# A scan step of 22 rounds in place of 23 in a two-layer attention and RWKV kernel

## The chip, the cores and the metric

The kernel runs on one core of a Trainium2 chip. The metric is the device time in microseconds (us) of one launch; a figure for a kernel is the median of several launches. The engines are TensorE (PE for matmuls, PEld for its weight loads), VectorE (DVE), ScalarE (ACT), GpSimd (POOL) and SyncE (SP), each working through its own list in order; between them stand semaphores. Matmuls write to eight banks of PSUM (`ps`), everything else lies in SBUF.

## What is computed

Two blocks follow each other over 1040 tokens of width 1024. The first has two layers, each with multi-head attention (4 heads), a bidirectional RWKV recurrence of 8 heads of 64, and a mixture of experts; the second has differential attention, a gated MLP and a dense feed-forward part. The change touches the recurrence alone:

```
def _wkv_scan(r, decay, k, v, kk, a, reverse):
    def step(S, inp):
        r_t, w_t, k_t, v_t, kk_t, b_t = inp
        sa = jnp.einsum('bhvk,bhk->bhv', S, kk_t)
        S = S * w_t[:, :, None, :] - sa[..., None] * b_t[:, :, None, :] + v_t[..., None] * k_t[:, :, None, :]
        return S, jnp.einsum('bhvk,bhk->bhv', S, r_t)
...
    def direction(d, wd, ad, reverse):
        wl = w0[d] + jnp.tanh(wd) @ w2[d]
        decay = jnp.exp(-jnp.exp(-jax.nn.softplus(-wl) - 0.5))
        a = jax.nn.sigmoid(a0[d] + ad @ a2[d])
        kd = heads(k * (1.0 + (a - 1.0) * k_a))
        y = _wkv_scan(rh, heads(decay), kd, vh, kk, heads(a), reverse)
        bonus = jnp.sum(rh * kd * r_k, -1, keepdims=True) * vh
        return y, bonus
```

It runs once forward (direction 0) and once backward (direction 1) in each layer, and the attention of the same layer is worked between its pieces.

## The kernel before

The recurrence is not run token by token. A step takes 104 tokens (two chunks of 52) of all 8 heads; `NT` is 10, so each direction has 10 steps. A step is cut into phases 0 to 31, written out for each engine in `scan_pe`, `scan_act`, `scan_dve` and `scan_pool`:

- phases 0 to 5: two small products (line 1366), tanh on ACT, on DVE the gate (L1541), the running sums (L1544), `cs` and `x1`; on POOL `a` and `b` (L1640, L1643);
- phases 6 to 10: on ACT the exponentials `ei`, `eK`, `ea` of the sums, on DVE `kr0`, `hb1`, `kr1`, products with them. On ACT phase 5 has the factor scaling "1+" (L1489, four instructions), which waits for POOL's `b`; POOL's `ak` (L1646) follows it;
- phase 11: TensorE turns `v` and `hb1` (`ps<-consts,u` and `ps<-consts,hb`), ACT takes them out of PSUM (`vT`, `hbT`), DVE makes `hb0`;
- phases 12 and 13: TensorE multiplies `kr` with `hb` (two banks each), DVE masks the results out of PSUM into `Ab` and `Ak`. The product of phase 12 goes to the banks that `vT` and `hbT` have left, that of phase 13 to those that `Ab` has left;
- phase 14: `hb0` is turned, and the bonus product `aa,rk`; phase 15 turns `lm` and makes T of level 0;
- phases 16 to 25: five levels. The even phase is `T,lm` on TensorE and then `XX` on DVE; the odd one is `XX,T` and `T,XX` on TensorE, and then T, half taken out by DVE (L1609), half by ACT. The next phase needs this each time;
- phases 26 to 31: the state of the two chunks (`S,kr`, `rh,T`, and the long product of 2.3 us), one after the other.

`PHASES` says which phases a round holds. A round is a stretch of code in which every engine does these phases of one direction, then the attention's share, then the phases of the other direction. Direction 1 lags by `STAGGER` = 11 rounds. A direction in its first four phases (rounds 0 to 3 of its step) stands last in the round, else direction 0 stands first:

```
    for n in range(STEPS * NT + STAGGER):
        turns_ = []
        for d in range(2):
            step, ph = divmod(n - STAGGER * d, STEPS)
            if 0 <= step < NT:
                turns_.append((ph < 4, d, step, PHASES[ph]))
        turns_.sort()
```

Rounds are counted below from 0 at the start of a step of direction 0. An attention item (one head, one tile of queries) spans six rounds, k = 0 to 5. On TensorE k = 0 is the larger part of the scores (`kn,qn`, `kpe,qp`; about 2.1 us), k = 1 the rest (0.7), k = 3 the turning of p (`consts,p`; 1.0), k = 4 the product with v (`v,pT`; 2.4). k = 1 has DVE's maxima (L1826), k = 2 three exponentials on ACT (L1811), k = 3 on DVE the taking out of pT (L1843), k = 5 on DVE the scaling `o` (L1851) and on ACT the square of it (L1815). Items start in the rounds `STARTS` = 2, 8, 13, 20 of a step of direction 0 in the first layer and in steps 0 and 5 of the second, and in `FEWER` = 2, 9, 17 in its other steps, always counted from `STEPS` times the step.

Of the kernel before, what the change touches and what calls it, by code (L numbers as in the profile page):

```python
# [9 lines left out]
ACT = mybir.ActivationFunctionType  # L10
# [268 lines left out]
def bc(ap, shape):  # L279
    return ap.to_broadcast(shape)  # L280
# [896 lines left out]

PHASES = [(0, 1, 2), (3, 4, 5), (6, 7, 9, 8, 10), (11,), (12,), (13, 14), (15,)] + [(ph,) for ph in range(16, 32)]  # L1180
STEPS = len(PHASES)
USES = 34
LEVELS = 6
# [35 lines left out]
def rounds():  # L1219
# [3 lines left out]
# [7 lines that stand above are left out]
# [9 lines left out]
def chunk(d, step):  # L1239
    i = step if d == 0 else NT - 1 - step  # L1240
    return slice(C * i, C * i + C)
# [11 lines left out]
def scan_bank(P, d, step, use):  # L1253
    return P.ps[2 * d + use % 2]
# [216 lines left out]
def scan_act(e, P, li, d, step, ph):  # L1471
    rw, pe, dv, ac, po = P.rw, P.c("scan_pe"), P.c("scan_dve"), P.c("scan_act"), P.c("scan_pool")
    m, sl, key = P.scan[d], chunk(d, step), (li, d, step)

    def take(out, view, use):
        e.wait_ge(*pe.at(*key, use))
        e.activation(out, view, ACT.Copy).then_inc(*ac.tick(*key, "ev", use))
# [5 lines left out]
        e.activation(m.aa, m.aa, ACT.Tanh, scale=0.5).then_inc(*ac.tick(*key, "aa"))  # L1483
    if ph == 11:
        take(m.vt[0:HP].rearrange("p c n -> p (c n)"), scan_bank(P, d, step, 2)[0:HP, :], 2)
    if ph == 5:
        e.wait_ge(*po.at(*key, "b"))
        for j in range(4):
            made = e.activation(m.aa[:, j, :], m.aa[:, j, :], ACT.Identity, bias=rw.par[:, 7, j:j + 1],  # L1489
                                scale=rw.par[:, 1, j:j + 1])  # L1490
        made.then_inc(*ac.tick(*key, "1+"))
    if ph == 6:
        e.wait_ge(*dv.at(*key, "x1"))
        e.activation(m.ei, m.cs if d == 0 else m.x1, ACT.Exp, scale=KAPPA).then_inc(*ac.tick(*key, "ei"))
# [2 lines left out]
            *ac.tick(*key, "eK"))  # L1497
    if ph == 8:
        e.activation(m.ea, m.cs if d == 0 else m.x1, ACT.Exp, scale=-KAPPA).then_inc(*ac.tick(*key, "ea"))
    if ph == 9:  # L1500
        e.wait_ge(*dv.at(*key, "f"))
        e.activation(m.f, m.f, ACT.Exp, scale=-0.5 * KAPPA).then_inc(*ac.tick(*key, "f"))
    if ph == 11:
# [25 lines left out]
def scan_dve(e, P, li, d, step, ph):  # L1529
    rw, pe, dv, ac, po = P.rw, P.c("scan_pe"), P.c("scan_dve"), P.c("scan_act"), P.c("scan_pool")  # L1530
    ident = bc(P.K["id52"][0:HP, :].unsqueeze(1), [HP, 8, H])
    m, sl, key = P.scan[d], chunk(d, step), (li, d, step)
# [29 lines left out]
        e.tensor_copy(m.old[:, (step + 1) % 2, :], total[:, :, m.chunks[1]]).then_inc(*dv.tick(*key, "old"))  # L1562
    if ph == 8:
        e.wait_ge(*ac.at(*key, "ei"))
        e.wait_ge(*po.at(*key, "ak"))
        e.scalar_tensor_tensor(m.hb[:, 1, :, :], m.hb[:, 1, :, :], -1.0, m.ei, ALU.mult, ALU.mult).then_inc(
            *dv.tick(*key, "hb1"))
    if ph == 9:
# [2 lines left out]
    if ph == 10:  # L1571
        e.wait_ge(*ac.at(*key, "ea"))
        e.tensor_tensor(m.kr[:, :, 1, :], rw.r[:, :, sl], m.ea, ALU.mult).then_inc(*dv.tick(*key, "kr1"))
    if ph == 11:
        e.tensor_tensor(m.hb[:, 0, :, :], m.aa, m.ei, ALU.mult).then_inc(*dv.tick(*key, "hb0"))
    if 12 <= ph < 14:
        dst = m.ab if ph == 12 else m.ak
# [57 lines left out]
def scan_pool(e, P, li, d, step, ph):  # L1635
    rw, pe, dv, ac, po = P.rw, P.c("scan_pe"), P.c("scan_dve"), P.c("scan_act"), P.c("scan_pool")
    m, sl, key = P.scan[d], chunk(d, step), (li, d, step)
    if ph == 2:
        e.wait_ge(*ac.at(*key, "aa"))
        e.tensor_scalar(m.aa, m.aa, 0.5, 0.5, ALU.mult, ALU.add).then_inc(*po.tick(*key, "a"))  # L1640
    if ph == 4:
        e.wait_ge(*po.at(*key, "a"))
        e.tensor_tensor(m.hb[:, 1, :, :], m.aa, rw.kk[:, :, sl], ALU.mult).then_inc(*po.tick(*key, "b"))  # L1643
    if ph == 7:
        e.wait_ge(*ac.at(*key, "1+"))
        e.tensor_tensor(m.aa, m.aa, rw.k[:, :, sl], ALU.mult).then_inc(*po.tick(*key, "ak"))  # L1646
    if ph == 11:
        e.wait_ge(*dv.at(*key, "hb0"))
        e.tensor_tensor(m.aa, rw.r[:, :, sl], m.aa, ALU.mult).then_inc(*po.tick(*key, "rka"))
    if ph in MASKS:  # L1650
        lv = MASKS[ph]
        if lv == 0:
            e.wait_ge(*dv.at(*key, "ev", 5))
        elif lv == 2:
            e.wait_ge(*dv.at(*key, "T", 0))
        elif lv > 2:
            e.wait_ge(*pe.at(*key, 8 + 3 * (lv - 2)))
        e.tensor_tensor(m.LM[lv % 2][0:HP], m.ab[0:HP, :, 0, :],  # L1658
                        bc(m.lmask[0:HP, H * lv:H * lv + H].unsqueeze(1), [HP, 8, H]), ALU.mult).then_inc(
            *po.tick(*key, "lm", lv))  # L1660
# [226 lines left out]
def recur_act(e, P, li):  # L1887
    for n, parts in groupby(rounds(), key=lambda x: x[0]):
        for _, part in parts:
            if part is None:  # L1890
                att_turned_act(e, P, li, n)
                att_act(e, P, li, n)
            else:
                scan_act(e, P, li, *part)
        close_head_act(e, P, li, n - STEPS * NT)
# [17 lines left out]
def recur_pool(e, P, li):  # L1913
    for n, part in rounds():
        if part is None:
            close_head_pool(e, P, li, n - STEPS * NT)
        else:
            scan_pool(e, P, li, *part)
# [2463 lines left out]
```

## Time and profile before

| | us |
|---|---|
| median of 3 runs (4924.06 to 4928.11) | 4927.36 |
| the profiled execution | 4924.1 |
| its span | 4921.9 |
| granted TensorE clock, mean share of full speed | 0.956 |
| PE busy over the span | 4475.2 (91%) |
| the scan of layer 0, about | 357 to 1070 |
| the scan of layer 1, about | 2193 to 2950 |

The profiled execution is 3.3 us faster than the median. The page gives busy times over the whole span, in which the two scans make up some 1470 us. In a timeline a matmul's end is modelled: a row of 32 matmuls of 0.60 us is followed by the next row 0.42 us after its start. A bracket behind a row gives the idle time of the engine before it, and what ended this.

### The profile page before, as it was taken

To read this page: it belongs to the slowest core of one execution; us is meant where nothing else is said; L and a number is where in the kernel's file an instruction comes from. 1 tells how busy PE (TensorE), PEld (TensorE's weight loads), DVE (VectorE), ACT (ScalarE), POOL (GpSimd) and SP (SyncE) were. 2 spreads that over 40 slices of the span, in tenths; PEclk is the share of its full clock that TensorE was granted. 3 is DMA by queue.
4 is the path that set the end of the run, shared out by engine and by line. 5 is a ranking of instruction groups with operands and counts; after the bars stand their busy time and mean duration, and the time that the engine had idled before them with its cause. 6 is when DMAs were issued, how large, how long until landed. Compare 5 with 4: busy or idle time off the path is not lost. (4 is left out here: it accounts for less than half of the span.)

```text
span 4921.9 us, 126091 instructions
## 1 busy us (share of the span) xinstructions
PE 4475.2 (91%) x55528; PEld 3810.2 (77%) x55528; DVE 3137.0 (64%) x4910; ACT 2160.1 (44%) x3962; POOL 1187.2 (24%) x863
## 2 busy tenths in 40 slices
PE   6989999989799968989999989799979988999999
PEld 6888888876588858878888877688857657888887
DVE  5436666669788874346656668788864475561752
ACT  2333443442288853433334342588843252331431
POOL 1002222222244420012222221354321000222221
PEclk9999999999799988999999999899989789999999
DMA  5421111123367664320111032566751003333332
GB/s 148 142 63 25 37 22 34 24 80 89 128 250 270 252 196 128 118 58 23 34 35 24 23 100 86 218 245 259 264 180 31 13 1 123 96 96 123 112 114 91
DMA packets 378285, 535.78 MB, mean 109 GB/s; under 512 B 117446, under 2 KB 301830, under 8 KB 349694
## 3 DMA queue, kind: packets, MB, share of 16 engines
q1 hardware_dynamic: 335645, 488.54, 30.7%
q0 software_dynamic: 40752, 33.95, 2.2%
q8 instruction: 440, 7.21, 0.6%
q10 hardware_dynamic: 1344, 5.24, 0.3%
q14 instruction: 104, 0.84, 0.1%
HBM read 569.43 MB, written 121.40 MB: 140 GB/s over the span
## 5 line engine op out<-in xcount | busy, mean ns | idle before, releaser
L289 PE MATMUL ps<-w_hi,xbT 128*128 128x512 f32 x1520 | 499.5, 400 | 19.8 <-DVE w L2838 19.8
L289 PE MATMUL ps<-hT,w_in 128*128 128x416 f32 (+1 forms) x2736 | 491.6, 338 | 4.1 <-DVE hT L3118 4.1
L289 PEld LDWEIGHTS ps<-hT,w_in 128*128 128x128 f32 x2736 | 455.6, 194 | 29.7 <-issue 19.2
L2838 DVE TENSOR_TENSOR w<-w,w_hi 128x2048 fp32r<-128x2048 f32 x190 | 425.4, 2278 | 2.2 <-issue 1.1
L1658 POOL TENSOR_TENSOR lm<-Ab,consts 116x416 f32<-116x416 f32 x240 | 254.3, 1071 | 472.6 <-PE ps L289 222.8
L289 PEld LDWEIGHTS ps<-w_hi,xbT 128*128 128x128 f32 x1520 | 289.1, 190 | 87.6 <-DVE w L2838 28.8
L2795 ACT ACTIVATE w_hi<-w 128x2048 fp32r<-128x2048 f32 x190 | 355.3, 1936 | 0.0
L289 PE MATMUL ps<-w,xbT 128*128 128x512 f32 x760 | 299.3, 394 | 0.0
L2869 DVE TENSOR_TENSOR w<-w,w_hi 128x2048 fp32r<-128x2048 f32 x95 | 221.7, 2333 | 95.5 <-ACT w_hi L2831 95.5
L289 PE MATMUL ps<-w_hi,actT 128*128 128x512 f32 x760 | 250.8, 391 | 5.0 <-DVE actT L2864 5.0
L289 PE MATMUL ps<-x1T,w_gate 128*128 128x512 f32 x1056 | 248.9, 392 | 3.0 <-DVE x1T L3805 1.6
L289 PE MATMUL ps<-x1T,w_up 128*128 128x512 f32 x1056 | 246.5, 389 | 0.0
L289 PE MATMUL ps<-w_down,act 128*128 128x512 f32 x1056 | 241.6, 391 | 3.0 <-POOL w_down L4031 3.0
L289 PEld LDWEIGHTS ps<-x1T,w_gate 128*128 128x128 f32 x1056 | 199.6, 189 | 45.5 <-issue 1.9
L289 PEld LDWEIGHTS ps<-w_down,act 128*128 128x128 f32 x1056 | 199.3, 189 | 45.0 <-POOL w_down L4031 3.4
L289 PEld LDWEIGHTS ps<-x1T,w_up 128*128 128x128 f32 x1056 | 198.2, 188 | 41.1
L289 PE MATMUL ps<-w_out,mixT 128*104 128x512 f32 (+1 forms) x864 | 220.2, 409 | 9.4 <-DVE w_out L2176 5.1
L1601 DVE TENSOR_TENSOR XX<-ps,consts 116x416 f32<-116x416 f32 x200 | 117.5, 587 | 172.4 <-PE ps L289 172.4
L4022 POOL TENSOR_TENSOR w_up<-w_up,w_up 128x1024 fp32r<-128x1024 f32 x44 | 116.4, 2645 | 459.5 <-ACT w_up L3944 459.5
L2784 POOL DMA_INDIRECT t_ys<-yo,slots x95 | 101.2, 1065 | 464.6 <-PE ps L296 374.1
L289 PEld LDWEIGHTS ps<-w_out,mixT 128*104 128x104 f32 (+1 forms) x864 | 152.6, 180 | 67.7 <-DVE w_out L2176 9.8
L795 POOL TENSOR_TENSOR w_in<-w_in,w_in 128x1024 fp32r<-128x1024 f32 x22 | 56.1, 2549 | 607.1 <-ACT w_in L810 607.1
(463 smaller groups left out, 10872.8 us busy)
## 6 DMA issues: line engine op xcount, KB each, us to landing
w<-in_moe_w_dram SPq DMA_DIRECT2D x192, 1024.0 KB
w_gate<-in_w_gate_dram SPq DMA_DIRECT2D x44, 512.0 KB, 3.8
w_up<-in_w_up_dram SPq DMA_DIRECT2D x44, 512.0 KB, 3.9
w_down<-in_w_down_dram SPq DMA_DIRECT2D x44, 512.0 KB, 3.6
w_in<-in_w_in_dram SPq DMA_DIRECT2D x36, 512.0 KB, 4.6
w_out<-in_w_out_dram SPq DMA_DIRECT2D x24, 512.0 KB, 7.4
t_h<-x SPq DMA_DIRECT2D x20, 416.0 KB
kn<-t_kn SPq DMA_DIRECT2D x8, 1040.0 KB, 6.7
```

Source lines behind the costliest of these rows:

```text
L289: made = e.matmul(out, a, b, start=start, stop=stop)
L795: e.tensor_tensor(w.lo, w.x, w.hf, ALU.subtract).then_inc(*count.tick(li, "lo", n))
L1601: e.tensor_tensor(m.XX[0:HP].rearrange("p (k u) t -> p k u t", k=2), both_banks(P, d, 0)[0:HP].rearrange("p k (u t) -> p k u t", t=H), bc( ...
L1658: e.tensor_tensor(m.LM[lv % 2][0:HP], m.ab[0:HP, :, 0, :], bc(m.lmask[0:HP, H * lv:H * lv + H].unsqueeze(1), [HP, 8, H]), ALU.mult).then_i ...
L2784: e.indirect_dma_start(T["ys"], bass.IndirectOffsetOnAxis(P.slots[:, table_column(b - 2):table_column(b - 2) + 1], 0), m.yo[b % 2], None, ...
L2795: e.activation(w.hi, w.x, ACT.Copy).then_inc(*P.c("moe_act").tick(li, "w13", b, k))
L2838: e.tensor_tensor(w.lo, w.x, w.hf, ALU.subtract).then_inc(*P.c("moe_dve").tick(li, "w13", b, k))
L2869: e.tensor_tensor(w.lo, w.x, w.hf, ALU.subtract).then_inc(*dv.tick(li, "w2", b))
L4022: e.tensor_tensor(w.lo, w.x, w.hf, ALU.subtract).then_inc(*po.tick(0, c, "lo", f))
```

## The change

`PHASES` puts phases 11 and 12 of a step into one round, so a step has 22 rounds and the whole scan of a layer 231 in place of 241. `STAGGER`, `STARTS` and `FEWER` stay as they are. On ACT the scaling "1+" moves from phase 5 behind the exponentials, to phase 10, and the exponential of `f` from phase 9 to 12. On DVE `hb1` waits for POOL's `b` and no longer for `ak`, and `hb0`, now in phase 12, waits for `ak`. POOL's `rka` moves to phase 12.

```diff
-PHASES = [(0, 1, 2), (3, 4, 5), (6, 7, 9, 8, 10), (11,), (12,), (13, 14), (15,)] + [(ph,) for ph in range(16, 32)]
+PHASES = [(0, 1, 2), (3, 4, 5), (6, 7, 9, 8, 10), (11, 12), (13, 14), (15,)] + [(ph,) for ph in range(16, 32)]
...
-    if ph == 5:
-        e.wait_ge(*po.at(*key, "b"))
-        for j in range(4):
-            made = e.activation(m.aa[:, j, :], m.aa[:, j, :], ACT.Identity, bias=rw.par[:, 7, j:j + 1],
-                                scale=rw.par[:, 1, j:j + 1])
-        made.then_inc(*ac.tick(*key, "1+"))
...
-    if ph == 9:
+    if ph == 10:
+        e.wait_ge(*po.at(*key, "b"))
+        for j in range(4):
+            made = e.activation(m.aa[:, j, :], m.aa[:, j, :], ACT.Identity, bias=rw.par[:, 7, j:j + 1],
+                                scale=rw.par[:, 1, j:j + 1])
+        made.then_inc(*ac.tick(*key, "1+"))
+    if ph == 12:
         e.wait_ge(*dv.at(*key, "f"))
         e.activation(m.f, m.f, ACT.Exp, scale=-0.5 * KAPPA).then_inc(*ac.tick(*key, "f"))
...
     if ph == 8:
         e.wait_ge(*ac.at(*key, "ei"))
-        e.wait_ge(*po.at(*key, "ak"))
+        e.wait_ge(*po.at(*key, "b"))
...
-    if ph == 11:
+    if ph == 12:
+        e.wait_ge(*po.at(*key, "ak"))
         e.tensor_tensor(m.hb[:, 0, :, :], m.aa, m.ei, ALU.mult).then_inc(*dv.tick(*key, "hb0"))
...
-    if ph == 11:
+    if ph == 12:
         e.wait_ge(*dv.at(*key, "hb0"))
         e.tensor_tensor(m.aa, rw.r[:, :, sl], m.aa, ALU.mult).then_inc(*po.tick(*key, "rka"))
```

With 22 rounds the item that starts in round 20 has its k = 2 to 5 in rounds 0 to 3 of the next step; before, k = 3 to 5 stood in rounds 0 to 2, and k = 2 in round 22. ScalarE's list at the start of direction 0's step in the first layer, before (`p` are the exponentials of k = 2, L1815 the square of k = 5, L1489 the scaling "1+"):

```order
L1811 ACTIVATE p125_174,stat127_176<-ps,stat127_176 104x416 x2
L1811 ACTIVATE p125_174,stat127_176<-ps,stat127_176 104x208
L1477 ACTIVATE T101_150<-ps 116x2x208
L1798 ACTIVATE pT126_175<-ps 104x2x104
L1481 ACTIVATE ps<-sig71_120 128x416
L1483 ACTIVATE aa74_123<-aa74_123 128x416
L1489 ACTIVATE aa74_123<-aa74_123,par11_60 128x104 x4
L1477 ACTIVATE T101_150<-ps 116x2x208
L1815 ACTIVATE pT126_175,mss5_54<-o129_178 104x128
L1494 ACTIVATE ei76_125<-cs72_121 128x416
L1496 ACTIVATE ps<-x73_122 128x416
```

The same place after:

```order
L1477 ACTIVATE T101_150<-ps 116x2x208
L1812 ACTIVATE p125_174,stat127_176<-ps,stat127_176 104x416 x2
L1812 ACTIVATE p125_174,stat127_176<-ps,stat127_176 104x208
L1481 ACTIVATE ps<-sig71_120 128x416
L1483 ACTIVATE aa74_123<-aa74_123 128x416
...
L1493 ACTIVATE ea75_124<-cs72_121 128x416
L1497 ACTIVATE aa74_123<-aa74_123,par11_60 128x104 x4
L1816 ACTIVATE pT126_175,mss5_54<-o129_178 104x128
L1477 ACTIVATE vT85_134<-ps 116x512
L1477 ACTIVATE hbT84_133<-ps 116x512
```

The exponentials of k = 2 moved from before the taking out of T to between it and the tanh, the scaling "1+" behind `ea`, and the square from before `ei` to directly before `vT`. TensorE's list behind the small products (L1366) of the same step, before:

```order
L1366 MATMUL ps<-u6_55,a213_62 128x104
L289 MATMUL ps<-T101_150,lm104_153 52x52 x16
L289 MATMUL ps<-v116_165,pT126_175 104x128 x10
L289 MATMUL ps<-XX102_151,T101_150 52x52 x16
...
L289 MATMUL ps<-consts0_49,hb83_132 52x64 x16
L289 MATMUL ps<-kr82_131,hb83_132 52x104 x16
L289 MATMUL ps<-T101_150,XX102_151 52x52 x16
L289 MATMUL ps<-kr82_131,hb83_132 52x104 x16
```

And after:

```order
L1366 MATMUL ps<-u6_55,a213_62 128x104
L289 MATMUL ps<-T101_150,lm104_153 52x52 x16
L296 MATMUL ps<-consts0_49,p125_174 104x104 x10
L289 MATMUL ps<-XX102_151,T101_150 52x52 x16
...
L289 MATMUL ps<-consts0_49,hb83_132 52x64 x16
L289 MATMUL ps<-kr82_131,hb83_132 52x104 x32
L289 MATMUL ps<-consts0_49,hb83_132 52x64 x16
L289 MATMUL ps<-aa74_123,rk814_63 8x104 x4
L289 MATMUL ps<-T101_150,XX102_151 52x52 x16
```

Between `T,lm` and `XX,T` of the other direction there stood `v,pT`, and now the turning of p; the two products of `kr` and `hb` now follow each other.

## Rows read from the trace of the kernel before

**Rows 1.** Both scans: us, busy PE PEld DVE ACT POOL, PEclk, DMA share, GB/s.
```profile
357.00:1070.00 713.00, 654.96 (x19132) 590.61 (x19131) 454.49 (x1083) 295.56 (x825) 196.42 (x196) 0.99 0.15 34
2193.00:2950.00 757.00, 677.78 (x19883) 614.78 (x19881) 476.46 (x1070) 300.54 (x814) 210.20 (x205) 0.97 0.17 43
```

**Rows 2.** Timeline, TensorE, layer 0, one step: start, us, idle before.
```profile
570.50 0.60 PE L289 MATMUL ps<-XX,T 52*52 52x52 f32 x32 [0.72 <-DVE XX L1601]
580.04 0.60 PE L289 MATMUL ps<-T,lm 52*52 52x52 f32 x32 [0.55 <-ACT T L1477]
581.80 1.10 PE L289 MATMUL ps<-consts,u 64*52 64x64 f32 x32 [0.49 <-DVE kr L1570]
586.39 1.63 PE L289 MATMUL ps<-kr,hb 64*52 64x104 f32 x32 [0.59 <-DVE Ab L1581]
620.38 0.60 PE L289 MATMUL ps<-T,XX 52*52 52x52 f32 x32 [0.34 <-DVE XX L1601]
624.38 0.82 PE L289 MATMUL ps<-consts,hb 64*52 64x64 f32 x22 [0.80 <-DVE Ak L1581]
630.95 0.60 PE L289 MATMUL ps<-T,lm 52*52 52x52 f32 x31 [0.56 <-ACT uu L1477]
643.47 0.60 PE L289 MATMUL ps<-XX,T 52*52 52x52 f32 x32 [0.73 <-DVE XX L1601]
```

**Rows 3.** Timeline, layer 0, rounds 0 to 2 of direction 0.
```profile
569.71 0.60 ACT L1811 ACTIVATE p<-ps,stat 104x416 f32<-104x416 f32 x1
...
571.20 0.22 ACT L1811 ACTIVATION_READ_ACCUMULATOR p<-ps,stat 104x1 f32 x1
571.42 1.10 PE L296 MATMUL ps<-consts,p 104*104 104x104 f32 x10
572.45 0.35 PE L1366 MATMUL ps<-u,w 64*128 64x104 f32 x1
574.06 2.43 PE L289 MATMUL ps<-v,pT 104*104 104x128 f32 x20
574.25 0.52 ACT L1481 ACTIVATE ps<-sig 128x416 f32<-128x416 f32 x1 [1.29 <-DVE sig L1537]
575.31 0.58 DVE L1601 TENSOR_TENSOR XX<-ps,consts 116x416 f32<-116x416 f32 x1
581.16 0.59 DVE L1570 TENSOR_TENSOR kr<-kk,ps 128x416 f32<-128x416 f32 x1 [1.93 <-ACT ps L1496]
585.16 0.58 DVE L1575 TENSOR_TENSOR hb<-aa,ei 128x416 f32<-128x416 f32 x1
```

**Rows 4.** Timeline, layer 1: the same waits where little stands between.
```profile
2803.70 0.35 PE L1366 MATMUL ps<-u,w 64*128 64x104 f32 x1
2808.69 2.50 PE L289 MATMUL ps<-v,pT 104*128 104x128 f32 x20 [0.80 <-DVE pT L1843]
2814.42 0.31 ACT L1815 ACTIVATE pT<-o 128x128 f32<-128x128 f32 x1 [1.27 <-DVE o L1851]
2815.45 1.54 PE L289 MATMUL ps<-kr,hb 64*52 64x104 f32 x30 [0.39 <-ACT vT L1477]
2820.71 0.33 PE L289 MATMUL ps<-S,kr 64*52 64x64 f32 x8
2843.17 0.60 PE L289 MATMUL ps<-XX,T 52*52 52x52 f32 x32 [1.82 <-DVE XX L1601]
```

**Rows 5.** Windows of 2 us in layer 1, columns as in rows 1.
```profile
2770.00:2772.00 2.00, 0.63 (x32) 0.48 (x28) 1.91 (x4) 1.05 (x2) 0.30 (x1) 1.00 0.37 86
2774.00:2776.00 2.00, 2.00 (x8) 1.72 (x6) 1.29 (x5) 1.65 (x5) 0.32 (x1) 0.50 0.00 0
```

**Rows 6.** Line 1615 and a timeline: the shrinking of S, and POOL beside it.
```profile
L1615 DVE TENSOR_TENSOR S<-S,f x76: 411/425/1021, 411.4 to 2937.2; 128x256 f32<-128x256 f32 x76
544.83 1.07 POOL L1649 TENSOR_TENSOR aa<-u,aa 128x416 f32<-128x416 f32 x1 [4.84 <-DVE hb L1575]
545.17 1.01 DVE L1615 TENSOR_TENSOR S<-S,f 128x256 f32<-128x256 f32 x1
```

## The prediction, made before the changed kernel ran

> **What bounds the kernel now.** I read the windows over the two scans first. TensorE is busy 654.96 of 713 us in layer 0 and 677.78 of 757 us in layer 1, no other engine more than two thirds [rows 1]. The change alters no arithmetic, so all it can win or lose is TensorE's waiting: 58 and 79 us. A round as such costs nothing; what costs is a place where TensorE reaches a product whose input is not yet there. So I read TensorE's timeline of one step of layer 0 for its gaps next. There are seven, and they come back one step of 73.0 us later (570.50, 643.47), 4.05 us together [rows 2]. In direction 0's rounds 0 to 4: `XX,T` directly behind its own `T,lm` (0.72), `T,lm` on ScalarE's half of T (0.55), the turning of v on `kr0` (0.49), the second `kr,hb` on `Ab` (0.59). In direction 1's: `T,XX` (0.34), the turning of `hb0` on `Ak` (0.80), and `T,lm` (0.56), whose releaser is named `uu` but which waits for T of level 0. A gap costs some 0.18 more than it shows, since a row of 0.60 is followed by the next 0.42 after its start. Then I read the other engines' lists for what arrives last at each.
>
> **What goes.** Direction 0's half: ScalarE no longer sits on the scaling "1+" in front of T and `ei`. `kr0` waited 1.93 us for `eK` [rows 3]; all of the 0.55 and the 0.49 go. The gap on `Ab` stays in part: `Ab` follows `hb0` 4.0 us behind `kr0` (581.16 to 585.16) through VectorE's maxima, and `T,XX` no longer stands in front to cover it; I take 0.2 for what is left. With 0.18 for each gap this is 0.73 + 0.67 + 0.57 = 2.0. Direction 1's half: `T,XX` now has 3.5 us of its partner's products in front and loses its 0.34; `Ak` no longer stands behind the taking out of pT, since k = 3 has slid one round away (0.80 goes); `T,lm` gets `v,pT` in front (0.56 goes). With 0.18 each: 2.2. Against it, this half takes over what direction 0 has now: `kr0` late by 0.4, because the square of k = 5 stands in front of `ei` there, and `Ab` late by 0.5, with 0.3 for the first `kr,hb`, which now starts as soon as ScalarE has emptied its banks. Net -1.0 us.
>
> **What is added, layer 0.** STARTS doesn't move, so the item that starts in round 20 slides by a round against direction 0's next step, and this has three costs, in each of 9 steps.
> First, round 0. The tanh waits for the sums only: from the start of the small products to it are 1.80 us (572.45, 574.25), to `XX` 2.86 and its end 3.44 [rows 3]. Now the three exponentials stand between T and the tanh. They take 1.71 us (569.71 to 571.42) and T ends 0.65 behind the start of the small products, so the tanh starts at 2.41, and `XX` ends at 4.05. TensorE reaches `v,pT` 1.61 behind the small products' start (574.06), and now has only the turning of p there (1.03, from 571.42 to 572.45) in place of 2.4 us: 2.64. It stands 4.1 - 2.64 = 1.46. The same wait is there in layer 1 where nothing at all is in front: 1.82 [rows 4].
> Second, round 3. The square of k = 5 now stands directly before `vT`, and waits for `o`, which VectorE makes behind the maxima of k = 1, behind `XX` and S. Counted from the small products: `XX,T` starts at 4.1; it takes 2.9 with the larger scores (576.5, where `v,pT` ends, to 580.04 less its gap of 0.73), to 7.0; `v,pT` to 9.4, `T,lm` and k = 1 another 1.2 (580.04 to 581.80 less 0.5), the turning of v and `hb1` 1.9 (581.80 to 583.7): TensorE is ready for `kr,hb` at 12.5. VectorE starts `XX` when `T,lm` is through, at 10.4. From `kr0` to `hb0` it takes 4.0 us [rows 3], 1.5 of them for the three products in front of `XX`: 2.5 behind it, at 12.9, the maxima are done. Then `o` 0.34, the square with its read 0.42, `vT` 0.6, and the bank is free at 14.3: 1.8 us. This queue exists already in layer 1: the square waits 1.27 for `o`, and `kr,hb` 0.39 for `vT` [rows 4].
> Third, round 5. VectorE now has phase 15 before the taking out of pT, so `v,pT` finds it not ready. In layer 1 it does so at 0.80 [rows 4]; I take 0.8. Beside these, 0.3 since k = 1 now delays `XX` at the step's end, 0.4 for exponentials behind the bonus product in round 4. Sum 4.8, less 2.0: +2.8 us a step.
> Thin covers: `T,lm` of direction 1's phase 18 side has only 0.5 us of work in front where it had `kn,qn`, and twice a `T,lm` of 0.42 stands where 0.9 stood. These are worth 0.45 and 0.25, +0.7 a step.
> Layer 0: 9 x 2.8 - 10 x 1.0 + 9.5 x 0.7 = 25.2 - 10 + 6.7 = +22 us.
>
> **Layer 1.** Eight steps have three items. Direction 0's half keeps its 1.82, the rest wins 0.9 (ScalarE's chain is 1.55 shorter, `T,XX` moved back) and gives 0.7 back at `v,pT`: -0.2. Direction 1's half gets the exponentials behind T (tanh 0.6 later), `XX,T` in front of `v,pT` and not behind it, and the square before `vT` with the scaling and `ak` in front of `hb0`. From the small products to the first S product it takes 17.0 us now; I lay it out row by row as above to 18.1, though a product pair of 0.95 has left that stretch: +2.05, less 0.4 for a pT wait that goes. Thin covers add 0.9. Sum 8 x (-0.2 + 1.65 + 0.9) = 19, and two steps behind four-item ones have layer 0's new places, 2 x 2.8, less 1.5 for their other half. Layer 1: +23 us.
>
> **Two smaller terms.** S shrinks in 425 ns by the median and up to 1021; the long one at 545.17 lies under a POOL product of 1.07 [rows 6]. POOL's `ak` now falls on S in all three kinds of half step, with VectorE's chain to `o` or `Ab` behind it. Between 0 and 0.6 us at 25 places, 0 to 15: I take 5, since POOL's product needs to cover only part. The Trainium skill (GPSIMD Engine Reference, "Specifications") has the two engines share SBUF interfaces, with contention for VectorE instructions of two SBUF inputs; S times `f` is one. By that rule the term is 15 and the sum 10 us higher; the row agrees, the median of 425 says that the overlap is what decides.
> The clock: behind a stretch in which TensorE worked 0.63 of 2 us the granted clock was 0.50 for a while (1.2 GHz) [rows 5]. Such stretches become more frequent by the two new waits of 1.5 and 1.8 us. In layer 1 ScalarE's chain hid the slow stretch. I take 4 us, bounds 0 and 20. [...]
>
> **The sum.** 22 + 23 + 5 + 4 = +54. Against the profiled execution, 4924.1 + 54 = 4978; the median stands 3.3 above it: 4981 us. Its own range: the layer terms, 45, between half and 1.2 times, since each wait was laid out from rows of other rounds, and the small terms between 0 and 35: 4927 + 22 = 4949 to 4927 + 54 + 35 = 5016.
>
> **Rivals.** *The waits go and their heirs don't come* (faster). If the square and the exponentials find their inputs early enough, the three costs in layer 0 (1.46 + 1.8 + 0.8 = 4.1) fall away, and direction 1's 1.65 in layer 1: 22 - 9 x 4.1 = -15, 23 - 8 x 1.65 - 8 = +2, thin covers halved -6: about -20, 4907 us. For it speaks that all three removed waits are seen in the trace and the new ones derived; it decides at whether `o` is ready before the turned `hb1` leaves TensorE, 12.5 against 13.2 here. Chance 0.14.
> *Every round costs the same* (faster): 10 rounds fewer of 713/241 = 3.0 us in each layer would be -60, 4867. Against it speaks the 92% of rows 1. Chance 0.02.
> *Slower by the clock and the port* (as forecast, larger): all bounds at the top, 5016 and above. Chance 0.06, counted in the forecast's.
> *Half of the new waits* (no change): if only round 0's and round 5's come and `vT` is in time, layer 0 is +6 and layer 1 about 0, other terms 0 to 5: 4927 to 4937. Chance 0.10 that it is within 0.2% (4917.5 to 4937.2), about what a measurement of this kernel can tell from no change.
> *Slower*, the forecast: 0.74. I put faster at 0.16. The range that leaves two in ten out cuts off the faster cases (below 4917) and the top above 5012: 4917 to 5012. Of the forecast's own cases, none near its centre rests on one term alone: `vT` alone is worth 16 us.
>
> **What would show it.** Right: in layer 0 the seven gaps become others: none on ScalarE's T and on `kr` in direction 0's half, but `XX,T` with 1.2 to 1.5 us on `XX`, the first `kr,hb` with about 1.6 on `vT`, `v,pT` with 0.5 to 0.8 on pT; ScalarE idle before L1816 for `o`; a step of layer 0 of 75 to 76 us where 73.0 stand now. Wrong: a first `kr,hb` without a gap, or `o` before the maxima. The whole forecast is wrong if TensorE's busy time in the scans changes by more than 10 us, which would be another mechanism.

## The result and the profile after

| | before | after |
|---|---|---|
| median, us (4 launches each, in turn) | 4927.73 | 5014.91 |
| ratio, 95% interval | | 1.0183 (1.0165 to 1.020) |
| the profiled execution | 4924.1 | 5026.55 |
| granted TensorE clock, mean | 0.956 | 0.951 |
| PE busy over the span | 4475.2 | 4512.0 |
| first to last L1544 of layer 0 | 692.2 | 740.6 |
| from there to layer 1's first | 1141.9 | 1160.2 |
| first to last L1544 of layer 1 | 683.3 | 718.0 |

The change made the kernel slower by 1.8%, 87 us by the medians, where +54 was forecast. The sign was right, and 5014.9 lies 3 us above the range. L1544, the running sums on VectorE, starts once in each step and direction, so its first and last start measure a scan without its tail. Its rows in the profile after, layer 0 and layer 1 (line: count, min/median/max ns, first and last start):

```profile
L1544 DVE TENSOR_TENSOR_SCAN ps<-consts,ps x20: 1019/1019/1028, 362.5 to 1103.1; 128x416 f32<-128x416 f32 x20
L1544 DVE TENSOR_TENSOR_SCAN ps<-consts,ps x20: 1017/1019/1028, 2263.3 to 2981.3; 128x416 f32<-128x416 f32 x20
```

So 48 us came in layer 0's scan, 35 in layer 1's and 18 between them; the profiled execution is the slowest of the four, 12 us above their median, so these three sum to more than 87. The windows over both scans, as in [rows 1]:

```profile
357.00:1125.00 768.00, 675.12 (x19304) 609.93 (x19306) 471.41 (x1090) 291.91 (x826) 198.73 (x198) 0.97 0.14 33
2260.00:3050.00 790.00, 685.75 (x19884) 623.49 (x19882) 488.84 (x1071) 296.71 (x812) 207.73 (x205) 0.96 0.16 41
```

In layer 0 TensorE is busy 20 us longer. The window holds 172 matmuls more, 1%, which is about 6 of the 20 us; the other 14 are the same work done slower, as the granted clock, 0.97 for 0.99, says too. TensorE's gaps over one step, to set against the seven of [rows 2]:

```profile
793.45 1.10 PE L289 MATMUL ps<-consts,u 64*52 64x64 f32 x32 [0.33 <-DVE kr L1570]
798.94 1.63 PE L289 MATMUL ps<-kr,hb 64*52 64x104 f32 x32 [1.49 <-DVE Ab L1582]
812.00 0.99 PE L289 MATMUL ps<-T,lm 52*52 52x52 f32 x31 [0.37 <-DVE T L1610]
820.53 0.60 PE L289 MATMUL ps<-XX,T 52*52 52x52 f32 x32 [0.81 <-DVE XX L1602]
825.30 0.60 PE L289 MATMUL ps<-XX,T 52*52 52x52 f32 x32 [1.14 <-DVE XX L1602]
836.37 4.62 PE L289 MATMUL ps<-kr,hb 64*52 64x104 f32 x64 [2.70 <-ACT vT L1477]
846.99 2.43 PE L289 MATMUL ps<-v,pT 104*104 104x128 f32 x20 [0.59 <-DVE pT L1844]
```

They are the gaps that were foretold, in their places: `kr` in direction 1's half, `XX` behind the exponentials, `vT` behind the square, `pT` in round 5. Five of the seven have the foretold size or less. Two don't: `kr,hb` on `vT` has 2.70 where 1.8 was laid out, and `kr,hb` on `Ab` 1.49 where 0.5 was. Both are 0.9 to 1.0 too long. And the products behind the first take 4.62 us for 64 where 3.33 is usual.

Two steps of the same kernel, side by side, show where the 0.9 is. Direction 0's round 3 at 674 us (columns: start, duration, engine):

```profile
674.26 1.06 POOL L1647 TENSOR_TENSOR aa<-aa,u 128x416 f32<-128x416 f32 x1 [4.63 <-ACT aa L1497]
674.30 1.31 DVE L1616 TENSOR_TENSOR S<-S,f 128x256 f32<-128x256 f32 x1
677.29 0.35 DVE L1852 TENSOR_SCALAR o<-ps,stat 104x128 f32<-104x128 f32 x1
677.67 0.31 ACT L1816 ACTIVATE pT<-o 104x128 f32<-104x128 f32 x1 [3.49 <-DVE o L1852]
677.98 0.58 ACT L1477 ACTIVATE vT<-ps 116x512 f32<-116x512 f32 x1
678.70 4.72 PE L289 MATMUL ps<-kr,hb 64*52 64x104 f32 x64 [2.69 <-ACT vT L1477]
```

And one step later, at 753 us, where VectorE's S started 0.03 us behind POOL's `ak` (L1647) by the profile and yet took the short time:

```profile
752.98 1.37 POOL L1647 TENSOR_TENSOR aa<-aa,u 128x416 f32<-128x416 f32 x1 [4.61 <-ACT aa L1497]
753.01 0.41 DVE L1616 TENSOR_TENSOR S<-S,f 128x256 f32<-128x256 f32 x1
755.49 0.31 ACT L1816 ACTIVATE pT<-o 104x128 f32<-104x128 f32 x1 [2.59 <-DVE o L1852]
756.52 3.33 PE L289 MATMUL ps<-kr,hb 64*52 64x104 f32 x64 [1.79 <-ACT vT L1477]
```

In the first, S (L1616) takes 1.31 us and ends 0.29 behind the end of `ak`. In the second S keeps its 0.41, and `ak` takes 1.37 in place of 1.06: here it was POOL that waited. The starts, 0.04 and 0.03 us apart, don't tell the two cases from each other; the durations do. The 0.90 of S comes back whole in the gap: 2.69 against 1.79. S is longer than 0.6 at 15 places in layer 0 and 17 in layer 1, at 1.31 or 1.32 in all but three of them; in the kernel before it was so at nine and seven places, and never above 1.02 [rows 6].

Those 16 places lay beside another POOL product, `rka` (L1649), beside which S no longer falls in the change; so the change put 32 long S in the place of 16. They also held the size of what came. `rka` has plainly begun first there, and S ends 0.28 us behind it, whether it began 0.34 behind (1.01, [rows 6]) or 0.68 (0.67), as in these two rows of the kernel before:

```profile
2378.04 1.07 POOL L1649 TENSOR_TENSOR aa<-u,aa 128x416 f32<-128x416 f32 x1 [3.92 <-DVE hb L1575]
2378.72 0.67 DVE L1615 TENSOR_TENSOR S<-S,f 128x256 f32<-128x256 f32 x1
```

An S that begins 0.03 behind a product of 1.06 takes 1.31 by the same reading. Windows of 2 us over the first of the two steps of the change (as [rows 5]):

```profile
676.00:678.00 2.00, 0.02 (x2) 0.00 (x0) 1.91 (x7) 0.33 (x3) 0.00 (x0) 1.00 0.00 0
678.00:680.00 2.00, 1.30 (x18) 1.33 (x20) 0.14 (x1) 1.14 (x4) 1.06 (x1) 0.73 0.38 89
680.00:682.00 2.00, 2.00 (x28) 2.00 (x26) 0.99 (x2) 0.00 (x0) 0.00 (x0) 0.50 0.16 31
```

Behind the idle 2.69 us the granted clock falls to 0.50 (1.2 GHz) until 683, and this makes 4.72 us of 3.33. So my reading of the profile alone was: one overlap of 0.90 us, twice a step, and a slow stretch behind the longer gap.

### The profile page after: what moved, and what is told of

It reads as the page before. It is cut to its first block and busy times, and to the rows that moved or that the text cites. A ratio compares the mean times of both kernels' runs of the same rounds, so it can differ in the third digit from the quotient of the medians.

```text
span 5024.4 us, 126091 instructions
## 1 busy us (share of the span) xinstructions
PE 4512.0 (90%) x55528; PEld 3844.3 (77%) x55528; DVE 3168.0 (63%) x4910; ACT 2154.3 (43%) x3962; POOL 1186.9 (24%) x863
## 5 line engine op out<-in xcount | busy, mean ns | idle before, releaser
L1610 DVE COPY T<-ps 116x416 f32<-116x416 f32 x160 | 94.3, 589 | 227.0 <-PE ps L289 226.9
L289 PE MATMUL ps<-kr,hb 64*52 64x104 f32 x2560 | 149.3, 272 | 63.4 <-ACT vT L1477 42.1
```

The source lines that it names most:

```text
L289: made = e.matmul(out, a, b, start=start, stop=stop)
L1610: e.tensor_copy(out, bank).then_inc(*dv.tick(*key, "ev", base + 1))
```

## Experiments

Fourteen kernels ran, in four groups. Each group has its own runs of the kernel before, whose median lay between 4919 and 4927, so they are compared by their ratio to it; "us over before" is the ratio taken of 4927.7. By it the change itself stands at +90 (87 by its medians). An interval of a ratio is 0.0010 to 0.0029 to either side, 5 to 14 us, mostly 7 to 10; a difference of two changed kernels is known to some 10 to 17. The last column is from one execution each, and the part ahead of layer 0's first L1544, which no edit touches, already varies between 357.6 and 362.5 us.

| kernel | ratio (95% interval) | us over before | scan of layer 0 / between / layer 1 |
|---|---|---|---|
| before | | 0 | 692.2 / 1141.9 / 683.3 |
| the change | 1.0183 (1.0165, 1.0200) | +90 | 740.6 / 1160.2 / 718.0 |
| S in phase 20 | 1.0107 (1.0078, 1.0135) | +53 | 714.6 / 1148.9 / 705.9 |
| `ak` behind S | 1.0117 (1.0101, 1.0134) | +58 | 721.3 / 1148.7 / 707.5 |
| `hb1` turned twice | 1.0165 (1.0140, 1.0190) | +81 | 738.8 / 1151.9 / 718.5 |
| STARTS with 19 | 1.0123 (1.0101, 1.0145) | +61 | 715.6 / 1142.4 / 720.4 |
| square last | 1.0067 (1.0041, 1.0093) | +33 | 710.6 / 1153.3 / 697.5 |
| merge alone | 1.0154 (1.0136, 1.0173) | +76 | 735.6 / 1155.5 / 719.0 |
| scaling alone, 23 rounds | 0.9968 (0.9954, 0.9982) | -16 | 690.3 / 1143.7 / 678.8 |
| before, S in phase 20 | 0.9965 (0.9951, 0.9979) | -17 | 685.4 / 1138.8 / 682.0 |
| before, square last | 0.9980 (0.9969, 0.9990) | -10 | 685.6 / 1141.6 / 688.3 |
| S in phase 20, STARTS with 19 | 1.0037 (1.0026, 1.0048) | +18 | 698.7 / 1139.4 / 700.7 |
| S in phase 20, square last | 1.0043 (1.0025, 1.0062) | +21 | 699.6 / 1148.6 / 694.3 |
| scaling alone, S in phase 20, 23 rounds | 0.9959 (0.9945, 0.9973) | -20 | 676.0 / 1141.5 / 671.1 |
| the same, square last | 0.9928 (0.9908, 0.9947) | -35 | 664.4 / 1141.0 / 672.5 |
| S in phase 20, STARTS with 19, square last | 0.9979 (0.9966, 0.9992) | -10 | 679.6 / 1142.3 / 685.4 |

### The overlap of S and ak

First S was taken out of POOL's way, by shrinking it four phases earlier.

```diff
-    if ph == 24 and step:
+    if ph == 20 and step:
```

> The changed kernel with one edit: VectorE shrinks the first S of a step in phase 20, not in phase 24, so that POOL's product ak no longer runs beside it. Theory P (the port): S takes 1.31 us beside ak and 0.41 alone, and 0.90 of this stands in front of the maxima, o and hb0. Then all S rows read about 0.42, the wait of kr,hb on vT in layer 0 falls from 2.70 to 1.79 and its wait on Ab from 1.49 to about 0.6, the granted clock stays at 1.00 behind them, and the time falls by some 9 x 0.9 + 10 x 0.9 in layer 0, 6 x 1.7 for slow stretches there, and 17 x 0.5 to 0.9 in layer 1: 35 to 42 us under the changed kernel, about 4975. Rival Q (order alone): the waits come from the order of the queues, the long S is hidden behind them: within 6 us of the changed kernel, vT still 2.7.

Measured 4976.5, 38 us under the change. The gap on `vT` fell to 1.47 and that on `Ab` to 0.25, and every `kr,hb` row that is whole has its 3.33 again:

```profile
891.97 3.33 PE L289 MATMUL ps<-kr,hb 64*52 64x104 f32 x64 [1.47 <-ACT vT L1477]
930.21 1.63 PE L289 MATMUL ps<-kr,hb 64*52 64x104 f32 x32 [0.25 <-DVE Ab L1582]
```

The gaps lost 1.23, not 0.90: S's own place in VectorE's list (0.34) went too. So this run doesn't price the overlap alone. The next one does, by leaving S where it is and making `ak` wait for it; `hb0` needs `ak` only two microseconds later.

```diff
     if ph == 7:
         e.wait_ge(*ac.at(*key, "1+"))
+        if step - (d == 0) >= 1:
+            e.wait_ge(*dv.at(li, 1 - d, step - (d == 0), "fS", 0))
```

> The changed kernel with one added wait: POOL's ak (phase 7) waits until VectorE has shrunk the other direction's first S, which stays in phase 24 in front of the maxima. The two no longer run side by side, and ak, which hb0 needs 2 us later, starts some 0.4 us later. Moving S to phase 20 took two things at once, the 0.90 of the overlap and S's own place (0.34 behind kr1); this run takes the overlap alone. Theory P (overlap 0.90, place 0.34 of the 1.24 by which both gaps fell): S at 0.42 in every row, vT 1.8, Ab 0.6, no slow stretch behind vT, and 26 to 30 us of the 38 under the changed kernel: 4985 to 4989. Rival (the place was most of it): S short, but the time above 5000.

Measured 4983.0, ratio 1.0117: 32 us under the change (20 to 44 by the two intervals), a little more than the 26 to 30 expected. S is short in all 76 rows, and both gaps have the size that the prediction had laid out:

```profile
L1616 DVE TENSOR_TENSOR S<-S,f x76: 411/424/426, 411.0 to 2995.0; 128x256 f32<-128x256 f32 x76
```

The timeline, `ak` first:

```profile
897.38 1.07 POOL L1649 TENSOR_TENSOR aa<-aa,u 128x416 f32<-128x416 f32 x1 [5.22 <-DVE S L1616]
900.33 3.33 PE L289 MATMUL ps<-kr,hb 64*52 64x104 f32 x64 [1.79 <-ACT vT L1477]
938.65 1.63 PE L289 MATMUL ps<-kr,hb 64*52 64x104 f32 x32 [0.59 <-DVE Ab L1582]
```

A wait that was added made the kernel 32 us faster. The same earlier S in the kernel before, as a measure of what it already bore:

> The kernel before with S in phase 20 as the only edit. Theory: S was long (1.01 or 0.67) at 16 places, 7 us of VectorE's time in all, less than half of it on the path: 2 to 5 us under the kernel before. Rival (nothing on the path): within 1 us of it. What it tells: how much of the port's cost the kernel before already bore, to set against the 38 us in the changed kernel.

Measured 4902.7, ratio 0.9965 (0.9951 to 0.9979), 17 us under before: a miss of mine, more than three times what I expected. The profile has 8 of them in the two scans (685.4 and 682.0 for 692.2 and 683.3); the others lie outside them, and I have no row that explains them. Four of them lie ahead of layer 0's first L1544 (357.6 for 361.8 us), where S has not yet run, so they are not the edit's.

So the 32 us are not all the change's. With S in phase 20 in both kernels the change costs 70 us by the ratios (+53 against -17) where it costs 90 with S in phase 24: it added some 20 of this kind, known only to within 18. By the two scans of the profiles it added 30 (38 fewer in the change, 8 in the kernel before).

### The slow stretch

To separate the clock from the gap that calls it, TensorE got work in the gap that nobody needs: `hb1` is turned twice in direction 0 of layer 0.

```diff
-        turns(e, P, [...]).then_inc(*pe.tick(*key, use))
+        for _ in range(2 if k and d == 0 and li == 0 else 1):
+            made = turns(e, P, [...])
+        made.then_inc(*pe.tick(*key, use))
```

> The changed kernel with one edit: in layer 0, direction 0, the turning of hb1 in phase 11 is issued twice, so that TensorE works 0.93 us longer in the gap in front of kr,hb, in which it has nothing to do. Nothing on the path gets shorter. Theory C (the clock answers to the gap): the gap falls from 2.69 to about 1.8, a length behind which no slow stretch was seen, so the granted clock stays at 1.00 in the six steps in which it fell, worth 6 x 1.7 = 10 us; 5 to 12 us under the changed kernel, between layer 0's first and last scan start. Rival (slow stretches come by chance or from the whole power of the core): as many stretches at 0.50 in layer 0 as before, the time within 3 us.

Measured 5010.4, 4.5 us under the change, with intervals that overlap, so the time alone shows nothing. The rows do. S is still long and `kr,hb` starts no earlier, but the gap reads 1.79 or 1.80 at all eight places, and no row behind it is slow:

```profile
674.50 3.33 PE L289 MATMUL ps<-kr,hb 64*52 64x104 f32 x64 [1.80 <-ACT vT L1479]
```

The window of 2 us that begins there keeps its clock of 1.00:

```profile
674.00:676.00 2.00, 1.50 (x32) 1.45 (x32) 0.54 (x1) 0.94 (x3) 1.06 (x1) 1.00 0.39 93
```

In the change itself five of six gaps of 2.68 to 2.70 have a row of 4.61 to 4.72 behind them. In this kernel and in the one with `ak` behind S none of the fifteen at 1.77 to 1.80 has. The merge alone (below) has gaps of 2.03 to 2.05 and both kinds of rows: two of its eight read 4.72. Each slow row costs 1.3 to 1.4 us, 7 us in layer 0. That the slow stretch goes with the gap in layer 0 is shown; that it is worth 7 us of the whole is worked out from the rows, and the scan doesn't bear it out: I had expected 5 to 12 us between layer 0's first and last L1544, and it is 1.8 (738.8 for 740.6), with S long at two places more, which cost about as much again. In layer 1 the rule is looser: of the change's eight gaps of 2.01 three have a row of 2.3 to 2.6 us behind them where 1.54 is usual, and a gap of 2.72 in this kernel (at 2713 us) has its usual row of 3.33 behind it.

### The item that slid

```diff
-STARTS = (2, 8, 13, 20)
+STARTS = (2, 8, 13, 19)
```

> The changed kernel with one edit: STARTS = (2, 8, 13, 19), so that the fourth item of a step has its k = 3 to 5 in rounds 0 to 2 as in the kernel before, and no longer k = 2 to 5 in rounds 0 to 3. Theory O (the slid item is the cost): the waits of XX,T on XX behind the exponentials (1.14 + 0.18), of kr,hb on vT behind the square (1.8 to 2.7 + 0.18) and of v,pT on pT (0.60 + 0.18) go from layer 0's nine steps and layer 1's two, and with them the slow stretches: 9 x 4.5 + 6 x 1.7 + 2 x 4 = 58 us at most, of which I expect 35 to 50 since k = 0 now stands nearer to k = 4 of the item before; about 4970. Rival (a wait that goes leaves an heir): under 15 us.

Measured 4983.8, 31 us under the change (30 by the ratios), a little less than the 35 to 50 that I expected. The waits on `vT` are gone from layer 0, but an heir took most of that place, since VectorE's chain with the long S now ends at `Ab`:

```profile
970.89 1.63 PE L289 MATMUL ps<-kr,hb 64*52 64x104 f32 x32 [1.88 <-DVE Ab L1582]
```

It also takes back what stood between the scans (1142.4 for 1160.2; the kernels with a slid item lie between 1148.6 and 1160.2, all others below 1144). One row of the change shows a part of what stands there: in the tail of layer 0, direction 1's `XX` comes behind VectorE's work on the closing's first tiles, `mix<-mix,yb` in 1.54 us next to a POOL product (0.69 without), and TensorE waits 3.93 us and runs slow behind it.

```profile
1139.61 1.06 POOL L1659 TENSOR_TENSOR lm<-Ab,consts 116x416 f32<-116x416 f32 x1 [5.90 <-PE ps L289]
1139.68 1.54 DVE L2304 TENSOR_TENSOR mix<-mix,yb 104x512 f32<-104x512 f32 x1
1143.43 0.95 PE L289 MATMUL ps<-XX,T 52*52 52x52 f32 x32 [3.93 <-DVE XX L1602]
```

With STARTS at 19 this wait is 2.29 us. The kernel with `ak` behind S has the same 3.93, and yet 1148.7 us between its scans where the change has 1160.2; what the other 11 us of the change's profile are stays open.

With the earlier S and STARTS together:

> The changed kernel with two edits together: S shrinks in phase 20 and STARTS = (2, 8, 13, 19). Theory: the port (38 us by e1_s_early) and the slid item (31 by e3_starts19, of which part was the port's too, since S delayed the square) are two causes that partly overlap: 4976 - 20 to 30 = 4946 to 4956, with a scan of layer 0 of about 692 us as in the kernel before, and one of layer 1 of 706 as in e1_s_early. Rival (22 rounds as such cost, whatever the item does): a scan of layer 0 above 705.

Measured 4939.7, ratio 1.0037 (1.0026 to 1.0048), +18 us: better than the sum that I had made, and the scan of layer 0 (698.7) stays below the 705 of the rival. The two causes are separate ones.

### The square in front of vT

ScalarE now does the square of k = 5 behind both directions' parts of its round.

```diff
-def att_act(e, P, li, n):
+def att_act(e, P, li, n, last=False):
...
     for k, item in att_turn(li, n):
+        if (k == 5) != last:
+            continue
...
                 scan_act(e, P, li, *part)
+        att_act(e, P, li, n, True)
         close_head_act(e, P, li, n - STEPS * NT)
```

> The changed kernel with one edit: ScalarE does the square of k = 5 at the end of its round, behind both directions' parts, so vT and hbT no longer stand behind it. Theory (an heir is close behind): the wait of kr,hb on vT (2.7, 9 times in layer 0, about 2.0 in direction 1's half of layer 1) goes; but the second kr,hb needs hb0 and the banks of Ab, which VectorE still makes behind maxima and o, so only 0.9 to 1.2 us of each is won, and the slow stretches (1.3 each, 6 times) go because the gap is cut in two: 9 x 1.0 + 8 + 8 x 1.0 = 15 to 28 us under the changed kernel. Rival (the square was the whole of it): 9 x 2.9 + 8 + 8 x 2.2 = 50 us under it.

Measured 4960.5, 54 us under the change: the rival's 50, and not my 15 to 28. My heir was too large. In direction 0's half 1.16 of the 2.70 is left, on `Ab`, where 1.5 to 1.8 was expected, the gap on `Ab` in direction 1's half fell too (0.85 for 1.49), that on `kr` vanished, because the square had stood before `ei` there, and in layer 1 nothing followed in place of `vT`'s 2.0.

```profile
893.58 1.63 PE L289 MATMUL ps<-kr,hb 64*52 64x104 f32 x32 [1.16 <-DVE Ab L1582]
930.05 1.63 PE L289 MATMUL ps<-kr,hb 64*52 64x104 f32 x32 [0.85 <-DVE Ab L1582]
```

So most of what the new order costs hangs on one short instruction (0.31 us) that waits for `o` in front of two that TensorE needs. In the kernel before it stood elsewhere:

> The kernel before with the square of k = 5 at the end of its round on ScalarE as the only edit. In the kernel before the square stands in front of ei in direction 0's half of layer 0 and before vT in layer 1 (0.39, eight times). Theory: the wait of kr0 on eK (0.49) is mostly the scaling 1+, so the square is worth 0.1 to 0.3 a step in layer 0 and 0.5 in layer 1: 4 to 8 us under the kernel before, against 40 to 54 in the changed one. Rival (square costs the same wherever it stands): 20 us or more.

Measured 4913.4, ratio 0.9980 (0.9969 to 0.9990), 10 us under before, 5 to 15 by the interval, where 4 to 8 was expected. The larger part of its cost is the change's.

With the earlier S as well:

> The changed kernel with S in phase 20 and the square last, STARTS as in the change (20). Theory: with the square gone from the chain the two kr,hb gaps of 1.16 and 0.85 are on Ab, and S is 0.90 of each: 9 x 0.9 + 10 x 0.75 in layer 0 and 17 x 0.5 to 0.7 in layer 1: 24 to 28 us under e7_square_last's 4960.5, so 4932 to 4937; against e1_s_early (4976.5) the square alone is then worth 40. Rival (port and square are one cost, whichever is taken first): within 8 us of 4960.

Measured 4938.5, ratio 1.0043 (1.0025 to 1.0062): 12 us under the kernel with the square alone by the ratios and 22 by the medians, whose reference lies 5 us lower in this group; the two scans are 14 us shorter in the profile (699.6 and 694.3). That is less than the 24 to 28 that I expected, and a difference that is known to some 16 us doesn't exclude the rival's 8. The rows speak for a cost of its own: the gaps on `Ab` of 1.16 and 0.85 are gone from layer 0. Whether the two costs share a part is not shown.

### The two parts of the change

> The kernel before with the merge alone: PHASES has (11, 12) in one round, 22 rounds a step; the scaling 1+ stays in phase 5 in front of the exponentials, hb1 waits for ak, hb0 and rka stay in phase 11, the exponential of f in phase 9. Theory (order terms as laid out in the prediction, and the port as e1_s_early priced it): the slid item's waits come as in the changed kernel, the gaps that the scaling's move took (1.7 to 2.0 a step in each layer) stay, but ak is no longer beside the first S of direction 0's half: 4976 (changed kernel without port) + 15 to 20 + about 5 for the 9 S that were long before: 4990 to 5003. S at 1.31 in none of direction 0's halves. Rival (the merge is harmless, the scaling's move did it): within 10 us of the kernel before.

Measured 5001.7, ratio 1.0154, +76 us. The merge is the slow part, and it is slow without the overlap: S is at 0.43 at most in all rows, the wait on `vT` at 2.0, as I read it because VectorE's chain starts later behind the scaling. Its gaps on ScalarE's T (0.56) and on `kr0` (0.49) are still those of [rows 2].

```profile
L1615 DVE TENSOR_TENSOR S<-S,f x76: 415/425/426, 412.5 to 3024.8; 128x256 f32<-128x256 f32 x76
```

TensorE's timeline:

```profile
910.58 4.72 PE L289 MATMUL ps<-kr,hb 64*52 64x104 f32 x64 [2.03 <-ACT vT L1477]
944.73 0.60 PE L289 MATMUL ps<-T,lm 52*52 52x52 f32 x32 [0.56 <-ACT T L1477]
946.49 1.10 PE L289 MATMUL ps<-consts,u 64*52 64x64 f32 x32 [0.49 <-DVE kr L1570]
```

The other part alone, in 23 rounds:

> The kernel before (23 rounds) with the ScalarE part of the change alone: the scaling 1+ moves from phase 5 behind the exponentials to phase 10, hb1 waits for b, hb0 (still phase 11) for ak. Theory: direction 0's half loses its three gaps (0.55, 0.49, part of 0.59, each with 0.18), 10 x 1.7 in layer 0 and less in layer 1, and the port takes back some: ak now runs beside S. Without the port -25, with it (19 + 17 places of 0.5 to 0.9, a third to two thirds of them on the path) -5 to +5: 4922 to 4933, S rows at 1.31 in more places than the 9 of the kernel before. If S stays at 0.42, 4903.

Measured 4911.5, ratio 0.9968, 16 us under before, where I had expected 5 us to either side. S is long at 24 places, but never above 1.16 us, and in layer 0 only beside `rka`, as before. At the eight places of layer 0 where `ak` falls on S, VectorE has begun 0.07 us earlier, and POOL waits:

```profile
579.68 0.41 DVE L1616 TENSOR_TENSOR S<-S,f 128x256 f32<-128x256 f32 x1
579.75 1.26 POOL L1647 TENSOR_TENSOR aa<-aa,u 128x416 f32<-128x416 f32 x1 [4.45 <-ACT aa L1497]
```

So the scaling's move wins 16 us by itself and loses 14 on top of the merge (+76 to +90). The difference is the overlap: take the 32 us of it away, and the move wins 18 there too (+76 to +58). The 14 and the 18 are known to within 12.

### What beats both

The scaling's move in 23 rounds, with S in phase 20:

> The kernel e4_scaling_23 (23 rounds, scaling 1+ behind the exponentials) with S shrunk in phase 20. Theory P: 24 S rows of 38 + 38 were long there (46.4 us together where 32 are needed), half to all of the 14 us on the path: 5 to 14 us under its 4911.5, so 4898 to 4906, faster than the kernel before by 0.4 to 0.6%. Rival (in 23 rounds the S is hidden): within 3 us of 4911.5.

Measured 4904.3, ratio 0.9959 (0.9945 to 0.9973): 7 us less by the medians and 4 by the ratios, which lies within the noise and doesn't exclude the rival. And with the square last:

> The kernel e8_scaling_early_23 (23 rounds, scaling behind the exponentials, S in phase 20) with the square of k = 5 at the end of its round on ScalarE. Theory: in layer 0 the square stands in front of ei, and the last gap on kr (0.31, 10 times, with 0.18 each) is its own; layer 1 has the wait on vT of 0.39 eight times: 5 + 4 us, so 4894 to 4900. Rival (TensorE's own work bounds it by now, the rest moves elsewhere): within 3 us of 4904.3.

Measured 4885.5, ratio 0.9928 (0.9908 to 0.9947): 0.7% faster than the kernel before, more than expected. In layer 0, a step from 857 us on has two gaps of some length left:

```profile
902.91 0.60 PE L289 MATMUL ps<-T,lm 52*52 52x52 f32 x31 [0.56 <-ACT uu L1477]
915.06 0.60 PE L289 MATMUL ps<-XX,T 52*52 52x52 f32 x32 [0.72 <-DVE XX L1602]
```

The 22 rounds with all three remedies (S, STARTS, square):

> The kernel e6_early_19 (22 rounds, S in phase 20, STARTS with 19) with the square of k = 5 at the end of its round. Theory: the gaps on kr (0.3, 19 times, with 0.18) and layer 1's on vT (0.8, 8 times) go: 9 + 8 us under 4939.7, so 4920 to 4928: 22 rounds come level with the kernel before, but stay 20 us or more above the 23 rounds with the same edits, because the merged round leaves v,pT on pT (0.60) and the scan's own chain no shorter. Rival (with all three costs gone the 22 rounds win): at or under 4900.

Measured 4907.2, ratio 0.9979 (0.9966 to 0.9992): faster than before, slower than the same edits in 23 rounds by 0.5%. The windows over the scan of layer 0 in the two kernels, of 23 and of 22 rounds:

```profile
361.00:1062.00 701.00, 665.26 (x19696) 603.79 (x19697) 462.53 (x1102) 296.43 (x839) 201.13 (x200) 0.99 0.15 35
361.00:1077.00 716.00, 674.84 (x19629) 608.98 (x19629) 463.12 (x1100) 296.89 (x836) 200.51 (x200) 0.98 0.15 35
```

Of these 15 us, ten are TensorE's busy time, at a clock of 0.98 for 0.99. Five are idle, and the wait of `v,pT` on pT (0.59, nine times), which the 23 rounds don't have, has their size. What lowers the clock there was not followed further.

## Why the prediction was off

By its own steps:

**What bounds the kernel.** Right: TensorE's gaps were the place to read. But "the change alters no arithmetic, so all it can win or lose is TensorE's waiting" was too narrow, since the same work took some 14 and 8 us longer in the two scans, through the clock. By my own last sentence, more than 10 us of busy time in the scans meant another mechanism. It did: not in place of the one laid out, but on top of it.

**What goes, and the sizes of the new waits.** Right. Direction 0's half lost its gaps on T and `kr0`; direction 1's took `kr` at 0.33 (0.4 foretold) and `T,lm` at 0.37 (0.45). `XX,T` has 1.14 (1.46), `v,pT` 0.60 (0.8). With `ak` behind S, `kr,hb` has 1.79 (1.8) and 0.59 (0.5). In layer 0's steps no wait on another engine came that had not been laid out; what did come is idle time without a releaser ("issue", 18.5 us over layer 0 for 11.4).

**The layer sums.** Nearly right. With `ak` behind S the scans are 29 and 24 us longer than before, where +22 and +23 were forecast. With S in phase 20 in both kernels, where neither bears an overlap worth counting, the difference is the same 29 and 24. The mean step of layer 0 (nine of them) went from 72.90 to 75.83, +2.9 for the forecast's 2.8 - 1.0 + 0.7 = 2.5.

**S and the port: the term that was mis-sized.** This is the step that failed: 5 us were taken for it, 15 were the bound; taking the overlap away gives 32 back. What the change added, over what the kernel before bore at its 16 places, is 20 by the ratios, known to within 18, and 30 by the scans, four to six times what was taken. Four things made the term small. I counted 25 places, and there are 32. I priced an overlap at 0.6, the longest in [rows 6], where S had begun 0.34 us behind POOL's product; beginning next to it, it loses 0.90. I let the overlap be partial ("needs to cover only part"), where S waits until the product has ended. And I set it beside the path, though S stands in VectorE's list directly before the maxima, `o` and `hb0`, the chain of my own two largest waits. Thirty-two places at 0.90 are 29 us. The page that I cited gives the contention without a size. The Trainium skill has the size elsewhere (SBUF — State Buffer, "SBUF: two separate sides"): the pair of ports is held for a whole instruction by whichever engine begins first, and the other stands still. The rows agree but for some 0.1 us: S takes 1.31 beside 1.06, where standing still to the end would make 1.44, and POOL 1.26 beside 0.41, where it would make 1.40. At 0.90 a place the bound for my 25 places would have been 22 us, and the range's top 5023; for the 32 that there are, 29 us and 5030.

**The clock.** 4 us were taken, 0 to 20. The five slow rows of layer 0 hold 7 by the rows, and the scan gave back 1.8 when they were gone. In the change they are not a term of their own there, since they come only behind gaps of 2.68 us or more, which S had made 0.9 longer, and not behind 1.8; the merge alone has two behind 2.03 and 2.05, with S short.

**Not in the sum.** 7 us between the scans (1148.7 with `ak` behind S, 1141.9 before), from the last item that slides past the end of layer 0's scan. I summed steps and left out the tail.

**The rivals.** None of the faster ones came, nor the unchanged one: one measurement can't say more of their chances. "Clock and port at the top" had 0.06 and is the nearest to what came, with the port's bound itself too low. The forecast's own range went to 5016 and still held the 5014.9; the one that was cut at 5012 didn't.

Together: 29 + 24 + 32 + 7 = 92, for +90 by the ratio. This is a tally and no test, since the 32 is itself a difference of two of these ratios; it only says that the profile with `ak` behind S (60) and its ratio (+58) agree.

## What to carry to other kernels

Before an instruction of POOL is moved, list what VectorE does at the new place, and price an overlap of two products with two SBUF inputs each at nearly the whole rest of the POOL one (0.90 of 1.03 us here, 0.60 of 0.73, 0.25 of 0.39), on the path if the VectorE one stands before anything that TensorE waits for. A wait between the two can be cheaper than letting them run side by side; here it was worth 32 us. A short instruction that waits for another engine belongs at the end of its engine's round, behind those that others wait for.

## What the runs showed of the hardware

- VectorE's S and POOL's `ak` or `rka`, elementwise products with two SBUF inputs each, kept each other waiting wherever they overlapped. S took 0.41 alone; where POOL's had begun first it ended 0.28 us behind it, in 0.67 us begun 0.68 behind, 1.01 begun 0.34 behind and 1.31 begun 0.03 behind. Where VectorE had begun 0.07 us earlier, S kept its 0.41 and POOL's took 1.26 in place of 1.06. VectorE's `XX` and the maxima, which read PSUM, kept their 0.58 and 1.36 (for three).
- In layer 0 TensorE's granted clock fell to 0.50 (1.2 GHz) behind five of six gaps of 2.7 us in the change, behind two of eight of 2.0 in the merge alone and behind none of fifteen of 1.8; a row of 64 products then took 4.6 to 4.7 us in place of 3.33. In the kernel that put useless products into the gap, which left 1.8 us of it, no row behind it was slow. That the whole got faster by it is not shown.
- Left open: what "issue" stands for in TensorE's gaps (up to 4.6 us in one piece, in the middle of a group of products). Its sum over layer 0 rose from 11.4 us before to 18.5 after; it is 16 to 19 in the other kernels of 22 rounds and 12 to 14 in the other ones of 23. None of these runs was aimed at it.
